# A two-layer decoder trunk on one core: the third down projection by halves, relu of one half on ScalarE, and steps moved between slots

## The chip, the core and the metric

The kernel runs on one core of one Trainium2 chip. The metric is the device time of one execution in microseconds (us). The kernel before took 1590.41 us as the median of three runs (1588.35 to 1590.41).

## What is computed

Two layers, each applied to a 512-token prompt and to 64 sampled tokens (8 sequences of 8), all in one pass over 576 columns. Everything is float32. Cut to what matters:

```
h = rms_norm(x, g_mix_pre)
proj = h @ w_in                      # 1024 -> 3584: queries, forget gates, values, gates of HGRN2; q, k, v of attention
rec, state = hgrn2(...)              # gated linear recurrence, 4 heads, chunks
att = dilated_attention(...)         # 8 heads, three (window, dilation) patterns, relative bias
x = x + rms_norm(concat(rec, att) @ w_out, g_mix_post)
h = rms_norm(x, g_mlp_pre)
u = square(relu(h @ w_up))           # 1024 -> 4096
x = x + rms_norm(u @ w_down, g_mlp_post)
```

Outputs: x of both groups after the last layer, the recurrent states, and the new rows of K and V.

## The kernel before, in words

Activations are transposed: features lie on the 128 partitions, tokens in the columns. The 576 tokens are cut in two halves of 320 and 256 columns, called half 0 and half 1 (`WIDE`). The weights come as blocks of 128x1024 float32 (512 KB). One block times one half gives one **output** of 128 features: 8 slices of 128 rows, each in three matmuls (high part of the weight, its rest, and the two parts of the activation), 24 matmuls in all, into one of two PSUM banks used in turn.

Each weight block passes a ring of four buffers (`RING`): SP loads it (`w_raw`), ScalarE copies it rounded (`high`, L770, tile `w_high`), VectorE subtracts (`rest`, L1400, tile `w_rest`); only the first blocks have their rest made elsewhere (GpSimd L694 for blocks 1 to 3). In steady state VectorE makes the rest of block v+4 right after the output that used block v, one output late.

The order of all work is written out by hand. `phases()` lists outputs in the order in which TensorE makes them; a layer is IA (input projection of half 0, 32 outputs), IB (half 1, 28 outputs, with OA, the output projection of half 0, in the middle), then the MLP. The MLP's 4096 hidden features are cut in four quarters: U0 to U3 are the up projections, D0 to D3 the down projections; A is half 0, B is half 1. The third down projection, D2, is done for both halves from one load of each block. The results of the D phases are summed in `acc[h]` (tile `reg`).

`steps_at()` hangs all other work on **slots**: slot (phase, i) is what every engine does after its part of output i. For each engine the program walks through the outputs and issues, per output, its eviction, the weight work and the slot's steps. So each engine's queue is in order, and a step that waits holds up what stands behind it. Steps that matter here:

- `norm_sum(k, h)`: sum over partitions on TensorE (L1109, ones), square root on ScalarE (L793), reciprocal on VectorE (L1424). k is 0 to 3: before the mixer, after it, before the MLP, after it.
- `post(k, h, p)`, p = 0 to 5: for two of eight slices, the projection's result times gain and norm (L1439), added to x (L1443); later p add up squares for the next norm (ScalarE L778, VectorE L1413).
- `pre(k, h, p)`: normalises x (L1455), rounds it (ScalarE L820 or L816, tile `h_high`), subtracts (L1467 or L1464, `h_rest`). For k = 2 the norm is left out here and multiplied in when the up projection is evicted.
- The eviction of an up output: VectorE, relu times the norm (L1497), then two squares on ScalarE (L872, L873) and a subtraction on VectorE (L1525). The norm factors of half 0 lie in `probs_s`, those of half 1 in `ks_tok` (`every_u`).
- `lev` and its helpers `q_odd`, `q_low`, `q_keep`, `q_rise`: levels of the recurrence (TensorE L1134, copies on ScalarE L890 and L897). `upd`: state update (VectorE L1664). `out`: the recurrence's output. `r_sum`, `r_spr`, `a_sum`, `a_spr`: norms per head (VectorE L1687, L1695). `sc`, `pt`, `pv`: attention (TensorE L1271, L1284, L1299).
- `x_sq`: squares of the input for the first norms. `f_scaled` (L1472): the first four outputs are made of x without its norm, and are multiplied by it afterwards.

## Time and profile before

| | |
|---|---|
| runs | 1588.35 to 1590.41 us, median 1590.41 |
| profiled execution, its own time | 1590.21 us |
| its span | 1588.4 us |
| what lies around the span | 1.8 us |
| TensorE matmul busy | 1535.0 us (97%) |
| VectorE busy | 1026.7 us (65%) |
| ScalarE busy | 806.6 us (51%) |
| DMA | 49% of 16 engines, 156 GB/s |

Times in the trace count from the start of the span. A busy TensorE is not TensorE at its peak; the start of each output against the next one tells whether it lost time.

### The profile page before, as it was taken

The page shows a single profiled execution, that of the slowest core. Times are in us where ns is not written, and L with a number is a line of the kernel's source. Part 1 is how long each engine was busy: PE and PEld are TensorE (multiplying, and loading weights), DVE is VectorE, ACT ScalarE, POOL GpSimd, SP SyncE. Part 2 cuts the span into 40 slices and gives each one's busy share as a digit, 9 for nine tenths or more (in the row PEclk, how much of TensorE's full clock was granted, in tenths as well). Part 3 has the DMA queues.
Part 4 walks back from the last instruction along what each step waited for, and adds up shares of the span by engine and source line. Part 5 has one row for each costly group of instructions (what it writes and reads, how often), then busy time and mean ns, then how long its engine had stood idle before and what let it go on. Part 6 is the DMA issues. An engine that isn't in the chain of part 4 may idle for free.

```text
span 1588.4 us, 29820 instructions
## 1 busy us (share of the span) xinstructions
PE 1535.0 (97%) x11984; PEld 1462.6 (92%) x11984; DVE 1026.7 (65%) x1784; ACT 806.6 (51%) x1424; POOL 124.6 (8%) x164
## 2 busy tenths in 40 slices
PE   6899999999999999999899999999999999999996
PEld 5898779998999999999899987899889999999996
DVE  6783777765558655445987656877555675653576
ACT  6545655476454644234664565546654454441442
POOL 3120123000000000000002100330000000000000
PEclk9999999999999999999999999999999999999998
DMA  5544664353454556334543467345434546652443
GB/s 202 187 152 164 216 224 130 123 179 107 133 170 147 172 181 183 119 107 146 160 146 120 139 214 260 127 145 159 153 93 147 160 153 182 184 172 80 138 154 113
DMA packets 83236, 247.88 MB, mean 156 GB/s; under 512 B 8691, under 2 KB 26483, under 8 KB 82972
## 3 DMA queue, kind: packets, MB, share of 16 engines
q1 hardware_dynamic: 83100, 245.98, 49.0%
q8 instruction: 96, 1.57, 0.4%
q14 instruction: 40, 0.33, 0.1%
HBM read 234.13 MB, written 14.44 MB: 156 GB/s over the span
## 4 chain that ended last, share of the span: by engine, by line
PE 81%; DVE 10%; ACT 3%; DMA 3%; issue 2%; SPq 1%; DVEq 0%; ACTq 0%
PE ps L1074 66%; PE ps L1071 6%; PE ps L1134 3%; DVE w_rest L1400 2%; DMA kc<-kcT 2%; PE ps L1284 1%; DVE reg L1439 1%; PE ps L1271 1%; PE ps L1299 1%; ACT w_high L770 1%; DVE x L1443 1%; DMA bias<-rel_scratch 1%; DVE square_sum L1413 1%; DVE norm_every L1424 1%; DVE s_in L1676 0%
## 5 line engine op out<-in xcount | busy, mean ns | idle before, releaser
L1074 PE MATMUL ps<-h_high,w_rest 128*128 128x320 f32 (+1 forms) x1888 | 569.4, 302 | 8.8 <-DVE w_rest L1400 4.7
L1074 PE MATMUL ps<-h_rest,w_high 128*128 128x320 f32 (+1 forms) x1888 | 559.8, 296 | 0.0
L1074 PE MATMUL ps<-h_high,w_high 128*128 128x320 f32 (+1 forms) x1888 | 559.7, 296 | 0.0
L770 ACT ACTIVATE w_high<-w_raw 128x1024 fp32r<-128x1024 f32 x384 | 402.1, 1051 | 224.1 <-PE ps L1074 223.2
L1400 DVE TENSOR_TENSOR w_rest<-w_raw,w_high 128x1024 fp32r<-128x1024 f32 x380 | 471.4, 1245 | 33.9 <-ACT w_high L770 33.8
L1074 PEld LDWEIGHTS ps<-h_high,w_rest 128*128 128x128 f32 x1888 | 359.6, 190 | 23.8 <-issue 14.1
L1074 PEld LDWEIGHTS ps<-h_rest,w_high 128*128 128x128 f32 x1888 | 359.8, 191 | 0.4
L1074 PEld LDWEIGHTS ps<-h_high,w_high 128*128 128x128 f32 x1888 | 359.5, 190 | 0.0
L1074 PE MATMUL ps<-u_high,w_rest 128*128 128x320 f32 (+1 forms) x1024 | 305.8, 299 | 3.8 <-DVE u_rest L1525 2.0
L1074 PE MATMUL ps<-u_high,w_high 128*128 128x320 f32 (+1 forms) x1024 | 303.4, 296 | 0.0
L1074 PE MATMUL ps<-u_rest,w_high 128*128 128x320 f32 (+1 forms) x1024 | 303.4, 296 | 0.0
L1074 PEld LDWEIGHTS ps<-u_high,w_rest 128*128 128x128 f32 x1024 | 194.8, 190 | 7.0 <-issue 4.2
L1074 PEld LDWEIGHTS ps<-u_rest,w_high 128*128 128x128 f32 x1024 | 194.8, 190 | 0.1
L1074 PEld LDWEIGHTS ps<-u_high,w_high 128*128 128x128 f32 x1024 | 194.7, 190 | 0.0
L872 ACT ACTIVATE tmp<-tmp 128x256 f32<-128x256 f32 (+1 forms) x128 | 57.0, 445 | 190.7 <-DVE tmp L1497 190.5
L1507 DVE TENSOR_TENSOR reg<-reg,ps 128x320 f32<-128x320 f32 (+1 forms) x96 | 43.5, 453 | 137.7 <-PE ps L1074 137.5
L1071 PE MATMUL ps<-w_rest,h_high 128*128 128x256 f32 (+1 forms) x320 | 93.9, 293 | 3.4 <-ACT key L857 2.7
L1497 DVE SCALAR_TENSOR_TENSOR tmp<-ps,probs_s 128x320 f32<-128x320 f32 x64 | 31.4, 490 | 94.3 <-PE ps L1074 94.3
L1071 PE MATMUL ps<-w_high,h_rest 128*128 128x256 f32 (+1 forms) x320 | 90.0, 281 | 0.0
L1071 PE MATMUL ps<-w_high,h_high 128*128 128x256 f32 (+1 forms) x320 | 90.0, 281 | 0.0
L1071 PEld LDWEIGHTS ps<-w_rest,h_high 128*128 128x128 f32 (+1 forms) x320 | 57.4, 179 | 7.7 <-issue 5.5
L1727 DVE CUSTOM_DVE_ANT_0 prob<-ps,bias 128x128 f32<-128x128 f32 (+3 forms) x64 | 28.7, 487 | 54.7 <-PE ps L1271 38.2
(203 smaller groups left out, 1673.8 us busy)
## 6 DMA issues: line engine op xcount, KB each, us to landing
w_raw<-w SPq DMA_DIRECT2D x384, 512.0 KB, 3.6
...
```

What stands on the lines that cost most here:

```text
L770: A.activation(whi[:, v % RING], raw[:, v % RING], ACT.Copy).then_inc(S["w_hi"], 1)
L872: A.activation(tmp[:, 2 + k % 2, 0:n], tmp[:, s, 0:n], ACT.Square)
L1071: last = pe.matmul(ps[0:rows, bank, 0:256].rearrange("p (s n) -> p s n", s=2), xt[:, c, t0:t0 + rows], wt[:, slot:slot + 2, c, :], **flags)
L1074: last = pe.matmul(ps[:, bank, 0:n], wt[:, slot, c, :], xt[:, c, :], **flags)
L1134: last = pe.matmul(ps[:, 3 + i, 256 * c:256 * c + 192].rearrange("p (z t) -> p z t", z=3), kb[h][:, 2 * g + i, pro(h, c)], qx[h][g][:, i, ...
L1271: last = pe.matmul(ps[:, 5 + s, b0 * P:(b0 + nb) * P], qa[h][r, j, pro(h, u % 2)], src[r, j, c0:c0 + nb * P], start=True, stop=True)
L1284: last = pe.transpose(dst, prob[h][:, s, j * P:j * P + P], ident)
L1299: last = pe.matmul(ps[DH * s:DH * s + DH, bank, c0:c0 + P], va[j // 2][:, j % 2, a * DH:a * DH + DH], pt[h][:, s, j * P:j * P + P], start= ...
L1400: V.tensor_tensor(wlo[:, v % RING], raw[:, v % RING], whi[:, v % RING].bitcast(F32), ALU.subtract).then_inc(S["w_lo_d"], 1)
L1497: V.scalar_tensor_tensor(tmp[:, gate_slot[o.n], 0:n], src, 0.0, every_u[o.h][:, 0:n], ALU.max, ALU.mult)\
L1507: V.tensor_tensor(dst, dst, src, ALU.add).then_inc(S["ev_d"], 1)
L1727: V.tensor_tensor_reduce(out=prob[h][:, s, 0:k], in0=ps[:, 5 + s, 0:k], in1=bias[h][j % 2][:, s, full - k:full], scale=1.0, scalar=-3.0e38 ...
```

## The change

1. **Phases.** U2B, D2, U3A, D3A, U3B, D3B become D2A, U3A, D3A, U2B, D2B, U3B, D3B. The eight blocks of D2 are loaded, rounded and subtracted twice per layer (400 blocks instead of 384). The last four phases belong to half 1 alone.
2. **The end of half 0's MLP.** `norm_sum(3,0)`, `post(3,0)`, `norm_sum(0,0)` and `pre(0,0)` are spread over these four phases, a step in every second slot, where they stood in every slot of U3B and D3B.
3. **Relu of half 1** goes to ScalarE (`ACT.Relu` from PSUM), without the norm; `pre(2,1)` normalises x on VectorE as for k = 0.
4. **Slots.** In IA, `norm_sum(0,1)` and `pre(0,1)` are issued behind the `q_` and `lev` steps of the same slot. In IB, `upd` of half 1 goes from slot 22 to 24 and `out` from 25 to 27. In D0A, `r_sum` and `r_spr` of half 1 start one slot later.
5. **The opening.** The square root's table is loaded ahead of the first squares by a dummy activation. Block 6 is rounded earlier (`N_SOON` 3). Outputs 2 and 3 are multiplied by the norm, and the rests of blocks 5 and 6 made, ahead of the forget gates' work. GpSimd makes no `h_rest` any more; VectorE does all. The squares of half 1's input move from slots 1 to 4 to slots 8 to 11.

```diff
-N_SOON = 2
+N_SOON = 3
...
-                                  ("U2B", "U", 2, (1,)), ("D2", "D", 2, (0, 1)), ("U3A", "U", 3, (0,)), ("D3A", "D", 3, (0,)),
-                                  ("U3B", "U", 3, (1,)), ("D3B", "D", 3, (1,))):
+                                  ("D2A", "D", 2, (0,)), ("U3A", "U", 3, (0,)), ("D3A", "D", 3, (0,)),
+                                  ("U2B", "U", 2, (1,)), ("D2B", "D", 2, (1,)), ("U3B", "U", 3, (1,)), ("D3B", "D", 3, (1,))):
...
-    put("IB", 22, "upd", 1)
+    put("IB", 24, "upd", 1)
-    put("IB", 25, "out", 1)
+    put("IB", 27, "out", 1)
...
-    put("D0A", 0, "r_sum", 1)
-    put("D0A", 1, "r_spr", 1, 0)
-    put("D0A", 2, "r_spr", 1, 1)
+    put("D0A", 1, "r_sum", 1)
+    put("D0A", 2, "r_spr", 1, 0)
+    put("D0A", 3, "r_spr", 1, 1)
...
-    put("U3B", 1, "norm_sum", 3, 0)
+    span = [(ph, i) for ph in ("U2B", "D2B", "U3B", "D3B") for i in range(KC)]
+    put(*span[1], "norm_sum", 3, 0)
     for p in range(6):
-        put("U3B", 2 + p, "post", 3, 0, p)
-    put("D3B", 1, "norm_sum", 0, 0)
+        put(*span[3 + 2 * p], "post", 3, 0, p)
+    put(*span[16], "norm_sum", 0, 0)
     for p in range(5):
-        put("D3B", 2 + p, "pre", 0, 0, p)
+        put(*span[18 + 2 * p], "pre", 0, 0, p)
...
+        if 8 <= o.i < 12:
+            here.append(("x_sq", 0, 1, o.i - 8))
...
-            for c in range(1, KC, 2):
-                pool.wait_ge(S["h_hi"], c + 1)
-                V.tensor_tensor(hl[0][:, c, :], first_x[:, c, :], hh[0][:, c, :].bitcast(F32), ALU.subtract).then_inc(S["h_odd"], 1)
...
+                elif o.kind == "U":
+                    s = (gates[0] + ups[0]) % 2
+                    if uses[s]:
+                        act.wait_ge(*uses[s])
+                    A.activation(tmp[:, s, 0:n], src, ACT.Relu).then_inc(S["ev_a"], 1)
...
             high(1)
+            A.activation(rn[:, 0:1], eps[:], ACT.Sqrt)
             for p in range(4):
                 x_sq(0, 0, p)
...
-                if p in (1, 4):
-                    rest(RING + p // 4)
+                if p == 1:
+                    rest(RING)
+            for o in outs[2:N_FIRST]:
+                f_scaled(o)
+            rest(RING + 1)
+            rest(RING + 2)
```

Three places show how queues change. In the names, `reg_55` is half 0's register tile and `reg_61` half 1's.

**VectorE, opening**, from the first reciprocal on. Before:

```order
L1424 RECIPROCAL norm_every<-norm_every 128x320
L1472 TENSOR_TENSOR tmp<-ps,norm_every 128x320 x2
L1455 SCALAR_TENSOR_TENSOR first_x<-x,prm,norm_every 128x320 x4
L1467 TENSOR_TENSOR h_rest_54<-first_x,h_high_53 128x320
L1400 TENSOR_TENSOR w_rest<-w_raw,w_high 128x1024
L1455 SCALAR_TENSOR_TENSOR first_x<-x,prm,norm_every 128x320 x2
L1467 TENSOR_TENSOR h_rest_54<-first_x,h_high_53 128x320
L1455 SCALAR_TENSOR_TENSOR first_x<-x,prm,norm_every 128x320 x2
L1467 TENSOR_TENSOR h_rest_54<-first_x,h_high_53 128x320 x2
L1400 TENSOR_TENSOR w_rest<-w_raw,w_high 128x1024
L1543 TENSOR_TENSOR lbc<-lb 128x4
```

Now:

```order
L1428 RECIPROCAL norm_every<-norm_every 128x320
L1474 TENSOR_TENSOR tmp<-ps,norm_every 128x320 x2
L1459 SCALAR_TENSOR_TENSOR first_x<-x,prm,norm_every 128x320 x4
L1469 TENSOR_TENSOR h_rest_54<-first_x,h_high_53 128x320 x2
L1404 TENSOR_TENSOR w_rest<-w_raw,w_high 128x1024
L1459 SCALAR_TENSOR_TENSOR first_x<-x,prm,norm_every 128x320 x2
L1469 TENSOR_TENSOR h_rest_54<-first_x,h_high_53 128x320 x2
L1459 SCALAR_TENSOR_TENSOR first_x<-x,prm,norm_every 128x320 x2
L1469 TENSOR_TENSOR h_rest_54<-first_x,h_high_53 128x320 x4
L1474 TENSOR_TENSOR tmp<-ps,norm_every 128x320 x2
L1404 TENSOR_TENSOR w_rest<-w_raw,w_high 128x1024 x2
```

The four subtractions of GpSimd have come in, and the last two rows hold the rests of blocks 5 and 6. Before, the rest of block 6 stood behind seven operations on `lbc` and `lb`, nine on three forget gates, three adds of squares, two copies and two `tmp` products.

**ScalarE, IA slots 13 to 15.** Before, then now:

```order
L820 ACTIVATE h_high_59<-reg_61 128x256 x2
L897 ACTIVATE q_mov_120<-reg_55 128x2x160
L890 ACTIVATE q_mov_119<-reg_55 128x2x128
L853 ACTIVATE reg_55<-ps 128x320
L770 ACTIVATE w_high<-w_raw 128x1024
```

```order
L893 ACTIVATE q_mov_119<-reg_55 128x2x128
L818 ACTIVATE h_high_59<-reg_61 128x256 x2
L856 ACTIVATE reg_55<-ps 128x320
L768 ACTIVATE w_high<-w_raw 128x1024
```

The copies into `q_mov`, for which `lev` waits, now stand ahead of the two roundings of `h_high`, which wait for VectorE's normalised x.

**VectorE, where half 0's `post(3,0)` begins.** Before (U3B), two slots:

```order
L1497 SCALAR_TENSOR_TENSOR tmp<-ps,ks_tok 128x256
L1400 TENSOR_TENSOR w_rest<-w_raw,w_high 128x1024
L1525 TENSOR_TENSOR u_rest_109<-tmp,u_high_107 128x256
L1439 SCALAR_TENSOR_TENSOR reg_55<-reg_55,prm,norm_every 128x320 x2
L1443 TENSOR_TENSOR x<-x,reg_55 128x320 x2
```

Now (U2B), two slots:

```order
L1404 TENSOR_TENSOR w_rest<-w_raw,w_high 128x1024
L1525 TENSOR_TENSOR u_rest_109<-tmp,u_high_107 128x256
L1443 SCALAR_TENSOR_TENSOR reg_55<-reg_55,prm,norm_every 128x320 x2
L1447 TENSOR_TENSOR x<-x,reg_55 128x320 x2
L1404 TENSOR_TENSOR w_rest<-w_raw,w_high 128x1024
L1525 TENSOR_TENSOR u_rest_109<-tmp,u_high_107 128x256
```

Before, every slot repeats all five rows; now the relu is gone from VectorE, and every second slot is without the `post`.

## Rows read from the trace of the kernel before

**Rows 1.** The page's first part: busy time, share of the span, instructions.
```profile
PE 1535.0 (97%) x11984; PEld 1462.6 (92%) x11984; DVE 1026.7 (65%) x1784; ACT 806.6 (51%) x1424; POOL 124.6 (8%) x164
```
**Rows 2.** TensorE's waits: line, whom it waited for, us in total, times, longest.
```profile
PE ps L1134 <- issue: 5.5, 8, 1.6
PE ps L1074 <- DVE w_rest L1400: 4.7, 1, 4.7
PE ps L1071 <- ACT key L857: 2.7, 2, 1.3
...
PE ps L1284 <- DVE reg L1695: 2.3, 2, 1.2
```
**Rows 3.** Stretches: length, busy PE, PEld, DVE, ACT, POOL, granted clock, DMA share, GB/s.
```profile
692.20:748.50 56.30, 56.30 (x386) 56.30 (x385) 30.00 (x44) 25.37 (x39) 0.00 (x0) 1.00 0.46 142
10.10:54.80 44.70, 36.73 (x199) 33.93 (x200) 36.35 (x69) 29.23 (x54) 14.15 (x9) 0.89 0.47 151
748.50:800.60 52.10, 48.11 (x390) 47.00 (x389) 48.09 (x85) 31.40 (x57) 0.00 (x0) 1.00 0.51 156
1526.00:1575.20 49.20, 47.59 (x388) 46.62 (x386) 36.47 (x62) 22.06 (x38) 0.00 (x0) 1.00 0.46 143
1303.30:1418.50 115.20, 115.20 (x962) 115.20 (x961) 70.46 (x104) 57.30 (x88) 0.00 (x0) 1.00 0.60 183
33.47:36.88 3.41, 3.27 (x12) 3.27 (x13) 3.13 (x9) 3.38 (x8) 0.95 (x1) 0.50 0.13 10
43.71:50.53 6.82, 5.22 (x19) 5.23 (x20) 6.42 (x14) 5.54 (x11) 0.00 (x0) 0.50 0.32 89
1166.70:1170.10 3.40, 3.40 (x15) 3.40 (x16) 0.48 (x1) 1.82 (x3) 1.28 (x1) 0.50 0.42 153
```
**Rows 4.** Timeline of the opening: start, us, engine, line, operation, tiles.
```profile
12.64 2.49 POOL L694 TENSOR_TENSOR w_rest<-w_raw,w_high 128x1024 fp32r<-128x1024 f32 x1 [10.39 <-ACT w_high L770]
...
13.25 2.24 DVE L1413 TENSOR_TENSOR square_sum<-squares 128x320 f32<-128x320 f32 x1 [0.38 <-ACT squares L778]
...
20.72 1.28 ACT L793 ACT_TABLE_LOAD   x1
...
22.58 2.15 DVE L1424 RECIPROCAL norm_every<-norm_every 128x320 f32<-128x320 f32 x1 [2.81 <-ACT norm_every L793]
...
25.57 1.93 DVE L1455 SCALAR_TENSOR_TENSOR first_x<-x,prm,norm_every 128x320 f32<-128x320 f32 x4
...
33.88 1.88 DVE L1400 TENSOR_TENSOR w_rest<-w_raw,w_high 128x1024 fp32r<-128x1024 f32 x1
...
44.04 1.22 DVE L1400 TENSOR_TENSOR w_rest<-w_raw,w_high 128x1024 fp32r<-128x1024 f32 x1
```
**Rows 5.** ScalarE's timeline in IA, first layer, slot 14.
```profile
89.79 0.81 ACT L820 ACTIVATE h_high<-reg 128x256 fp32r<-128x256 f32 x2 [2.44 <-DVE reg L1455]
```
**Rows 6.** Timeline in the second layer's IB, outputs 22 to 24.
```profile
1089.06 2.65 DVE L1664 SCALAR_TENSOR_TENSOR states<-states,f_tot,ps 128x128 f32<-128x128 f32 x8
...
1092.21 1.07 ACT L778 ACTIVATE squares<-x 128x320 f32<-128x320 f32 x2 [4.14 <-DVE square_sum L1413]
```
**Rows 7.** VectorE's timeline in U3B: the evictions of two neighbouring outputs.
```profile
762.66 0.42 DVE L1497 SCALAR_TENSOR_TENSOR tmp<-ps,ks_tok 128x256 f32<-128x256 f32 x1
...
766.19 0.42 DVE L1497 SCALAR_TENSOR_TENSOR tmp<-ps,ks_tok 128x256 f32<-128x256 f32 x1
```
**Rows 8.** Groups by line and form: busy us, mean ns | idle before.
```profile
L1109 PE MATMUL ps<-square_sum,ones 128*128 128x320 f32 x16 | 5.7, 437 | 0.7 <-DVE square_sum L1413 0.7
...
L857 ACT ACTIVATE key<-ps 128x256 f32<-128x256 f32 x8 | 3.0, 370 | 0.0
```
**Rows 9.** The page's costliest groups: weight rounding, weight rest, squares of up outputs.
```profile
L770 ACT ACTIVATE w_high<-w_raw 128x1024 fp32r<-128x1024 f32 x384 | 402.1, 1051 | 224.1 <-PE ps L1074 223.2
L1400 DVE TENSOR_TENSOR w_rest<-w_raw,w_high 128x1024 fp32r<-128x1024 f32 x380 | 471.4, 1245 | 33.9 <-ACT w_high L770 33.8
...
L872 ACT ACTIVATE tmp<-tmp 128x256 f32<-128x256 f32 (+1 forms) x128 | 57.0, 445 | 190.7 <-DVE tmp L1497 190.5
```

More of the change, by code:

```diff
@@ L99, in schedule @@
                 for j, (kind, h, k, tile) in enumerate(made):
-                    ev = EVICT[kind]
+                    ev = "a" if kind == "U" and h else EVICT[kind]
                     count[ev] += 1
@@ L117, in steps_at @@
         put("IA", 1 + p, "post", 3, 1, p)
-    put("IA", 13, "norm_sum", 0, 1)
-    for p in range(5):
-        put("IA", 14 + 2 * p, "pre", 0, 1, p)
     for G in range(GROUPS):
@@ L130, in steps_at @@
             put("IA", 9 + 4 * G + 2 * g, "lev", 0, G, g)
+    put("IA", 13, "norm_sum", 0, 1)
+    for p in range(5):
+        put("IA", 14 + 2 * p, "pre", 0, 1, p)
     put("IA", 18, "bias_in", 0, 0)
@@ L243, in steps_of @@
             if l == 0:
-                if name == "post" and which[2] < 4:
-                    here.append(("x_sq", 0, 1, which[2]))
                 continue
@@ L281, in scaled_before @@
     l, r = divmod(max(0, m - 2), 8)
-    return 8 * (m - 2 * l - (r > 1) - (r > 3))
+    return 8 * (m - l - (r > 1))
 def bank_of(o):
@@ L410, in build @@
     own_token = cst[:, 362:394]
-    every_u = [ps_s, kts]
+    every_u = ps_s
     def part(h, first):
@@ L788, in norm_sum @@
                 act.wait_ge(S["n_ms"], m + 1)
-                if k == 2:
-                    act.wait_ge(S["sp_t" if h == 0 else "su_done"], 4 * l + 4)
+                if (k, h) == (2, 0):
+                    act.wait_ge(S["sp_t"], 4 * l + 4)
                 elif m:
                     act.wait_ge(S["nap"], scaled_before(m))
-                A.activation((every_u[h] if k == 2 else every)[:, 0:WIDE[h]], ps[:, 7, 0:WIDE[h]], ACT.Sqrt, bias=eps[:], scale=1.0 / D)\
+                A.activation((every_u if (k, h) == (2, 0) else every)[:, 0:WIDE[h]], ps[:, 7, 0:WIDE[h]], ACT.Sqrt, bias=eps[:], scale=1.0 / D)\
                     .then_inc(S["n_root"], 1)
@@ L810, in pre @@
                 gain = prm[:, l, KC * k:KC * k + KC]
-                if k == 2 and p == 0:
-                    act.wait_ge(S["blk"], by[l, "OB" if h else "OA", KC - 1].n + 1)
+                if (k, h) == (2, 0) and p == 0:
+                    act.wait_ge(S["blk"], by[l, "OA", KC - 1].n + 1)
                 for c in (2 * p, 2 * p + 1):
-                    if k == 2:
+                    if (k, h) == (2, 0):
                         act.wait_ge(S["x_odd" if c % 2 else "x_even"], 4 * (4 * l + h) + p + 1)
@@ L828, in evict @@
                 src = ps[:, bank_of(o), 0:n]
-                if o.kind == "U":
+                if o.kind == "U" and o.h == 0:
                     return
@@ L867, in after @@
                     ups[0] += 1
-                    uses[s] = None
-                    act.wait_ge(S["ev_d"], o.evn)
+                    uses[s] = (S["u_sq"], ups[0])
+                    act.wait_ge(S["ev_a" if o.h else "ev_d"], o.evn)
                     if k >= 2:
@@ L1102, in _ @@
                      ("U0B", 0): normed, ("D0A", 0): upped, ("D0B", 0): upped, ("D1A", 0): upped, ("D1B", 0): upped,
-                     ("IA", N_FIRST): first_normed, ("D2", 0): upped, ("D2", 1): upped, ("D3A", 0): upped, ("D3B", 0): upped}
+                     ("IA", N_FIRST): first_normed, ("D2A", 0): upped, ("D2B", 0): upped, ("D3A", 0): upped, ("D3B", 0): upped}
             def norm_sum(l, k, h):
@@ L1421, in norm_sum @@
                 m, n = norm_no(l, k, h), WIDE[h]
-                to = (every_u[h] if k == 2 else every)[:, 0:n]
+                to = (every_u if (k, h) == (2, 0) else every)[:, 0:n]
                 dve.wait_ge(S["n_root"], m + 1)
@@ L1450, in pre @@
                 to = acc[h] if m else first_x
-                if p == 0 and k == 0:
+                if p == 0 and (k, h) != (2, 0):
                     dve.wait_ge(S["n_inv"], m + 1)
-                if p < 4 and k == 0:
+                if p < 4 and (k, h) != (2, 0):
                     for c in (2 * p, 2 * p + 1):
@@ L1458, in pre @@
                     for c in (2 * p - 2, 2 * p - 1):
-                        if m == 0 and c % 2:
-                            continue
                         dve.wait_ge(S["h_hi"], 8 * (4 * l + k + h) + c + 1)
                         done = S["h_odd" if c % 2 else "h_even"]
-                        if k == 2:
+                        if (k, h) == (2, 0):
                             V.scalar_tensor_tensor(hl[h][:, c, :], x[:, c, cols], gain[:, c:c + 1], hh[h][:, c, :].bitcast(F32),
@@ L1487, in evict @@
                     V.tensor_tensor(dst, src, tmp[:, gate_slot[o.n], 0:n], ALU.mult).then_inc(S["ev_d"], 1)
-                elif o.n in (2, 3):
-                    f_scaled(o)
-                elif o.kind == "U":
+                elif o.kind == "U" and o.h == 0:
                     k = n_up[0]
@@ L1496, in evict @@
                     dve.wait_ge(S["blk"], o.n + 1)
-                    V.scalar_tensor_tensor(tmp[:, gate_slot[o.n], 0:n], src, 0.0, every_u[o.h][:, 0:n], ALU.max, ALU.mult)\
+                    V.scalar_tensor_tensor(tmp[:, gate_slot[o.n], 0:n], src, 0.0, every_u[:, 0:n], ALU.max, ALU.mult)\
                         .then_inc(S["ev_d"], 1)
```

2 lines of the change are left out of this document (1 added, 1 removed).

## The prediction, made before the changed kernel had run

> **What bounds the kernel now.** The page's first part [rows 1] shows TensorE busy for 1535.0 us of 1588.4, VectorE 65%, ScalarE 51%. So a change counts only where TensorE now waits, or where it makes it wait. The next view is that of stretches [rows 3]. From 692.2 to 748.5, 16 outputs of half 0 take 56.3 us, 3.52 us each; from 1303.3 to 1418.5, 40 outputs of half 1 take 115.2 us, 2.88 us each, at full clock and 183 GB/s of loads. These two figures are the floor of an output: TensorE waits for nothing there. I hold every other stretch against them.
>
> Four kinds of places are above the floor. **The opening**: the first eight outputs take 44.7 us where the floor is 28.2, with one wait of 4.7 us for the rest of a weight block [rows 2, 3]. **Two places per layer in the mixer**: 1.6 us ahead of a `lev` (put down to issue; 5.5 us in 8 waits), and 1.3 us behind ScalarE's copy of a key (2.7 in 2) [rows 2]. **D0A**: 1.2 us behind `r_spr` on VectorE (2.3 in 2) [rows 2]. **U3B and D3B**: 52.1 us in the first layer and 49.2 in the second, where 16 outputs need 46.1 [rows 3]. There VectorE is busy 48.1 of 52.1 us. The clock is granted at 0.50, the lower level of 1.2 GHz, in three stretches of 3.4, 6.8 and 3.4 us [rows 3], each around a moment in which TensorE had been waiting (two in the opening, one in the second layer's D0A). At half clock half the time is lost: 5.1 us and 1.7 us.
>
> **The change part by part.**
>
> *The last four phases, 7.0 us.* In U3B a slot takes VectorE 3.53 us from one eviction to the next [rows 7] while TensorE needs 2.88: VectorE falls behind by 0.65 us in a slot, by 1 to 1.6 us where squares are added too, until the rests come late. Now the eviction (0.33 of it, by its record of 0.42 less the overlap with its neighbour) is ScalarE's, and the `post` stands in every second slot. The slot with it takes 3.2 us, the one without it 1.25 for the rest [rows 9] plus about 0.4 for the other subtraction, 1.65: 4.85 for two, 5.8 with two adds of squares of 0.48, where TensorE gives 5.76. VectorE just holds, with three outputs of reserve in the ring. So both stretches fall to the floor plus norm sums of 0.7 us each (5.7 us for 8 [rows 8]): 52.1 - 46.1 - 1.4 = 4.6 and 49.2 - 46.1 - 0.7 = 2.4. What is late next is nothing there; the tail after the last output keeps its chain.
>
> *Sixteen more block loads, nothing.* Each costs ScalarE 1.05 us and VectorE 1.25 us [rows 9]. They fall in D2A and D2B, where D2's outputs had a block for 6.4 us of TensorE. D2B then is like any B phase, whose 2.88 us per 512 KB block the stretch at 183 GB/s holds without a wait [rows 3]. Their cover is TensorE's own work; without it each would cost 1.25 us, 20 in all.
>
> *Relu on ScalarE, nothing.* It should last as long as the copy of a PSUM tile of the same form, 0.37 us [rows 8], against 0.42 on VectorE [rows 7]. ScalarE's turn in a half-1 up slot is then 1.05 + 0.37 + 2 x 0.45 = 2.3 us of 2.88 [rows 9], and 3.3 in every second slot of U2B with two squares more, 5.6 for two of 5.76. The step queued behind relu is the next block's rounding, needed three outputs later. The Trainium skill, "ScalarE: Activation LUTs", Rules for kernel authors, says to use VectorE for relu, per element up to about three times as fast in bf16; the float32 rows above show the two engines level, so here I leave it at nothing and keep the rule as a rival.
>
> *`pre(2,1)` normalised, nothing.* Eight products of about 0.48 us per layer on VectorE in U2A, four slots with 1.0 us more each. VectorE in comparable phases is busy 30.0 of 56.3 us [rows 3]. Bounds: 0 and 1 us per layer, if the last `h_rest` is late for U0B; the ring's reserve argues for 0.
>
> *`lev` ahead of `pre` in IA, 3.2 us.* ScalarE's roundings of `h_high` waited 2.44 us for VectorE and had the `q_mov` copies behind them [rows 5]; TensorE's wait of 1.6 us ended right after. With the copies first, they wait for nothing that is late. 2 x 1.6.
>
> *`upd` and `out` later in IB, 2.7 us.* The 2.65 us of state updates stood in front of the adds of squares, ScalarE's squares waited 4.14 us for these, and the key copy that frees TensorE's bank stood behind the squares [rows 6]. `upd` now comes behind the last of them. Gain between 0 (another wait in its place) and 2.7; I take 2.7, since slots 24 to 27 have less on VectorE.
>
> *`r_sum` and `r_spr` later in D0A, 4.0 us.* The last transposes (L1284) no longer stand behind the products that free their bank: 2.3 us [rows 2], and with the wait goes what I take to be the cause of the low clock from 1166.7 to 1170.1, worth 1.7 [rows 3].
>
> *The opening, 7.0 us.* The 1.28 us table load ahead of the square root at 20.72 goes [rows 4], so the reciprocal begins at 21.3 instead of 22.58. Where is the load now? Ahead of the first squares, which thereby come 1.3 us late. But the first add of squares, begun at 13.25, took 2.24 us and ended at 15.49, just after GpSimd's `w_rest` (12.64 to 15.13) [rows 4]: it did not get going earlier, and a start at 14.6 ends the same. The Trainium skill, "SBUF — State Buffer", section SBUF: two separate sides, calls this an exclusive lock on a port pair that VectorE and GpSimd share, held for a whole instruction; the trace agrees (2.24 us). Without such a lock the load would be paid and the opening gain 1.3 us less.
>
> From 21.3 on, VectorE's queue by the rows [rows 4]: reciprocal 2.15; two `tmp` and six more pieces of `first_x`, `h_rest` and `tmp` (8 `first_x`, 8 `h_rest`, 4 `tmp`, twenty operations, each taken at 1.93 / 4 = 0.48) 9.65; three block rests 3.75. The rest of block 5 is done at 35.6, of block 6 at 36.9. (Before: 35.8, and 45.3 for block 6, which is the wait of 4.7.) Four subtractions that were GpSimd's are in it. Output 5 runs from 35.6 at latest. If nothing else is late, outputs 5, 6 and 7 end at 35.6 + 3 x 3.52 = 46.1, where they ended at 54.8: 8.7 us. If the rest of block 7, behind 22 small operations, needs as long as the rest of block 6 did behind 23 (35.8 to 44.0, 8.3 us with its waits, and 1.25), it is there at 46.4, and the eighth output ends at 49.9: 4.9 us. I take 7.0. The low clocks are inside these times, except that TensorE again waits twice for over 1 us: one new stretch of 3.4 us at half clock would cost 1.7, and widens the low side. The squares moved to slots 8 to 11 lie under outputs with `lev` work between them; 0 to 1 us.
>
> **Sum**: 7.0 + 3.2 + 2.7 + 4.0 + 7.0 = 23.9 us. The profiled execution took 1590.2 us (span 1588.4 and 1.8 around it), 0.2 under the median of the runs, so the forecast is 1590.2 - 23.9, rounded to **1566 us**.
>
> **The rivals.**
>
> *The opening gives little* (20%). Its waits move to block 7 and the clock falls again. For: two waits of over 1 us remain by my own chain. Against: 4.9 us came out even with the long reading. With 1.5 instead of 7.0: 1571.5.
>
> *The mixer's waits come back behind the moved steps* (12%). `out` now stands right ahead of U0A, `r_spr` next to `a_sq`. Nothing is gained in IB and D0A, 6.7 us: 1573.
>
> *More than counted* (12%). VectorE is freer everywhere, and the records of neighbours overlap, so that my chains are long: 8.7 in the opening and some smaller waits: 1561.
>
> *Relu is slow on ScalarE* (3%). At three times VectorE's 0.42, 1.26 us, ScalarE's turn is 1.05 + 1.26 + 0.9 = 3.2 us, 0.33 over 2.88; 64 half-1 up outputs lose 21 us: 1587. The skill's rule, taken to the letter, is this case.
>
> *Slower* (4%). One mechanism: in the half-1 up phases ScalarE waits for VectorE's x and squares with the next output's relu queued behind, so that TensorE waits for its bank. It decides once ScalarE's turn, waits included, passes 2.88 us. At 3.35 us, 0.47 for 64 outputs, it costs 30 us, more than the 23.9: 1596. Against it: 0.6 us of room in the plain slots, and a reserve of one bank.
>
> *No change* (3%): the gains exist, but as waits that reappear before the MLP, whose floor they cannot lower: about 1590.
>
> *The forecast* has the remaining 46%. The range 1558 to 1577 takes in the first three rivals and the bounds above. A measurement of this kernel can tell 0.2%, 3 us, from no change. Faster by more than that: 0.93; within: 0.03; slower: 0.04.
>
> **What would show it.** The last four phases at 2.88 us per output and VectorE below 85% there, where it was 92%; no wait of 4.7 us on `w_rest`, and output 8 begun at 46 to 50 us instead of 54.8; no 1.6 us ahead of `lev`; no wait on `key` and `reg` L1695; granted clock 1.00 in D0A of the second layer. Wrong would be: waits on L1074 with ScalarE or VectorE named inside U0B to D1B, which have none now; or a low clock in a new place.

## The result

| | before | changed |
|---|---|---|
| runs | 1588.35 to 1590.41 us | 1569.68 to 1575.23 us |
| median of four runs each, same chip | 1589.87 us | 1570.07 us |
| profiled execution | 1590.21 us, span 1588.4 | 1569.68 us, span 1567.9 |

The ratio is 0.9887, with a 95% interval of 0.9867 to 0.9906. The span is 20.5 us shorter; the sum said 23.9. One execution of an experiment below took 2471.07 us, at a mean granted clock of 0.556; it is left out of every comparison.

The page's first part of the changed kernel answers to [rows 1]. ScalarE has 36.5 us more, TensorE 7.3 less.

```profile
PE 1527.7 (97%) x11984; PEld 1456.7 (93%) x11984; DVE 1031.7 (66%) x1756; ACT 843.1 (54%) x1501; POOL 120.7 (8%) x160
```

TensorE's waits after the change (line, whom it waited for, us in total, times, longest), against [rows 2]. The one of 4.7 us is gone, and so is that on `reg` L1695. New at the top stand two of 2.1 us on `w_rest` in L1075, a line that named ScalarE's `key` before; longer is only the wait of 10.3 us before the first output, which was 10.1 before.

```profile
PE ps L1075 <- DVE w_rest L1404: 4.3, 2, 2.1
PE ps L1138 <- issue: 3.1, 7, 0.9
PE ps L1078 <- DVE w_rest L1404: 2.4, 2, 1.3
...
PE ps L1318 <- DMA kc<-kcT: 1.6, 2, 1.2
...
PE ps L1366 <- ACT att_sq L993: 1.0, 2, 0.5
```

Stretches after the change (columns as in [rows 3]): the first eight outputs; the last four phases of layer 0; 16 outputs of U3B and D3B in layer 1; U0B to D1B in layer 1; D0A in layer 1; D2A in layer 1, where blocks are loaded that were shared before.

```profile
10.30:47.20 36.90, 32.93 (x199) 30.23 (x200) 31.09 (x66) 26.94 (x47) 8.43 (x5) 1.00 0.52 169
693.30:786.50 93.20, 93.20 (x775) 92.88 (x774) 73.28 (x112) 59.80 (x106) 0.00 (x0) 1.00 0.58 180
1508.60:1554.70 46.10, 46.10 (x385) 45.99 (x384) 24.98 (x35) 24.35 (x44) 0.00 (x0) 1.00 0.46 154
1285.30:1377.50 92.20, 92.20 (x771) 92.20 (x770) 51.71 (x65) 50.62 (x82) 0.00 (x0) 1.00 0.59 182
1136.90:1176.80 39.90, 39.41 (x308) 34.62 (x306) 21.99 (x37) 19.00 (x29) 3.87 (x3) 1.00 0.35 106
1377.50:1405.60 28.10, 28.10 (x194) 28.10 (x193) 12.93 (x16) 8.48 (x8) 0.00 (x0) 1.00 0.49 152
```

The last four phases take 2.91 us an output with VectorE at 79% (73.28 of 93.2), where U3B and D3B before had 3.26 and 92% [rows 3]. The granted clock is 1.00 in this execution until 1559.6 us; from there to the end it is 0.50, but TensorE has no work left (the kernel before has the same piece from 1579.7 us on).

Where the 20.5 us come from, by stretches between the starts of outputs in the two traces:

| stretch | before | changed | gain | forecast |
|---|---|---|---|---|
| IA, layer 0 | 149.6 | 140.8 | 8.8 | 7.0 + 1.6 |
| IA, layer 1 | 134.2 | 132.3 | 1.9 | 1.6 |
| IB slots 0 to 17, both layers | 199.5 | 198.7 | 0.8 | 0 |
| IB slots 18 to 27, both layers | 74.9 | 75.1 | -0.3 | 2.7 |
| U0A, both layers | 93.1 | 93.2 | -0.2 | 0 |
| D0A, layers 0 and 1 | 40.2 + 41.8 | 39.9 + 39.9 | 2.1 | 4.0 |
| U2B or D2A to D3B, layer 0 | 182.7 | 177.7 | 5.0 | 4.6 |
| the same, layer 1, with the tail | 192.9 | 190.4 | 2.5 | 2.4 |

All other phases agree within 0.1 us; the first output starts 0.1 us later. (Gains are taken before rounding.)

### The profile page after: what moved, and what is told of

It reads as the page before. It is cut to its first block, busy times and chain, and to the rows that moved or that the text cites. A ratio compares the mean times of both kernels' runs of the same rounds, so it can differ in the third digit from the quotient of the medians.

```text
span 1567.9 us, 29899 instructions
## 1 busy us (share of the span) xinstructions
PE 1527.7 (97%) x11984; PEld 1456.7 (93%) x11984; DVE 1031.7 (66%) x1756; ACT 843.1 (54%) x1501; POOL 120.7 (8%) x160
## 4 chain that ended last, share of the span: by engine, by line
PE 86%; DVE 8%; ACT 2%; DMA 2%; issue 1%; SPq 1%; DVEq 0%; ACTq 0%
PE ps L1078 68%; PE ps L1075 7%; PE ps L1138 3%; DVE w_rest L1404 2%; PE ps L1288 1%; PE ps L1303 1%; PE ps L1275 1%; DMA kc<-kcT 1%; DVE reg L1443 1%; ACT w_high L768 1%; DVE norm_every L1428 1%; DVE x L1447 1%; DVE s_in L1676 1%; DMA w_raw<-w 1%; PE ps L1193 0%
## 5 line engine op out<-in xcount | busy, mean ns | idle before, releaser
L768 ACT ACTIVATE w_high<-w_raw 128x1024 fp32r<-128x1024 f32 x400 | 419.0, 1052 | 208.9 <-PE ps L1078 206.5
L1404 DVE TENSOR_TENSOR w_rest<-w_raw,w_high 128x1024 fp32r<-128x1024 f32 x396 | 490.5, 1244 | 55.2 <-ACT w_high L768 55.1
L1078 PE MATMUL ps<-u_high,w_rest 128*128 128x256 f32 (+1 forms) x1024 | 304.9, 298 | 0.0
L1078 PE MATMUL ps<-u_high,w_high 128*128 128x256 f32 (+1 forms) x1024 | 303.1, 296 | 0.0
L1078 PE MATMUL ps<-u_rest,w_high 128*128 128x256 f32 (+1 forms) x1024 | 303.1, 296 | 0.0
L1075 PE MATMUL ps<-w_rest,h_high 128*128 128x256 f32 (+1 forms) x320 | 93.7, 293 | 4.3 <-DVE w_rest L1404 4.3
L1075 PE MATMUL ps<-w_high,h_rest 128*128 128x256 f32 (+1 forms) x320 | 90.0, 281 | 0.0
L1075 PE MATMUL ps<-w_high,h_high 128*128 128x256 f32 (+1 forms) x320 | 90.0, 281 | 0.0
L1525 DVE TENSOR_TENSOR u_rest<-tmp,u_high 128x256 fp32r<-128x256 f32 (+1 forms) x128 | 58.2, 455 | 38.3 <-ACT u_high L876 38.3
```

The source lines that it names most:

```text
L768: A.activation(whi[:, v % RING], raw[:, v % RING], ACT.Copy).then_inc(S["w_hi"], 1)
L1075: last = pe.matmul(ps[0:rows, bank, 0:256].rearrange("p (s n) -> p s n", s=2), xt[:, c, t0:t0 + rows], wt[:, slot:slot + 2, c, :], **flags)
L1078: last = pe.matmul(ps[:, bank, 0:n], wt[:, slot, c, :], xt[:, c, :], **flags)
L1404: V.tensor_tensor(wlo[:, v % RING], raw[:, v % RING], whi[:, v % RING].bitcast(F32), ALU.subtract).then_inc(S["w_lo_d"], 1)
L1525: V.tensor_tensor(ul[o.h][:, o.k, :], tmp[:, 2 + k % 2, 0:n], uh[o.h][:, o.k, :].bitcast(F32), ALU.subtract).then_inc(S["u_set"], 1)
```

## The experiments

The kernel before was run beside each experiment, and a ratio is to it. No experiment's interval lies apart from the changed kernel's, so the totals alone settle nothing. While TensorE has work, a granted clock of 0.50 shows in these traces in pieces of 3.4 us (once 6.8), none to four in one execution. So stretches of the traces are compared, and what a piece costs is named. The stretches repeat well: where D0A is not edited it takes 39.9 us in every layer of every compared trace of the new kernels.

### Relu and the spread, one without the other

All else as changed. First: the old phases, `post(3,0)` and `pre(0,0)` in every slot, with relu on ScalarE.

```diff
-                                  ("D2A", "D", 2, (0,)), ("U3A", "U", 3, (0,)), ("D3A", "D", 3, (0,)),
-                                  ("U2B", "U", 2, (1,)), ("D2B", "D", 2, (1,)), ("U3B", "U", 3, (1,)), ("D3B", "D", 3, (1,))):
+                                  ("U2B", "U", 2, (1,)), ("D2", "D", 2, (0, 1)), ("U3A", "U", 3, (0,)), ("D3A", "D", 3, (0,)),
+                                  ("U3B", "U", 3, (1,)), ("D3B", "D", 3, (1,))):
...
-        put(*span[3 + 2 * p], "post", 3, 0, p)
+        put("U3B", 2 + p, "post", 3, 0, p)
...
-        put(*span[18 + 2 * p], "pre", 0, 0, p)
+        put("D3B", 2 + p, "pre", 0, 0, p)
```

> The changed kernel (1570.1 us, span 1567.9) with the old phases: D2 for both halves from one load, post and pre of half 0 in every slot of U3B and D3B; relu stays on ScalarE. Theory A, spreading is what filled the gap in the last phases: a slot with post is 3.2 us of VectorE and 3.6 to 4.2 with adds of squares, against 2.88, on top of the reciprocal, so waits of 1 to 3 us per layer are back: span 1570 to 1573. Theory B, taking relu off VectorE was enough, since the ring holds a reserve of three outputs: span 1567.9 within 0.5, and 16 fewer block loads.

Second: the new phases, with relu and norm of half 1 on VectorE in one product.

```diff
-    A.activation(tmp[:, s, 0:n], src, ACT.Relu).then_inc(S["ev_a"], 1)
...
+    V.scalar_tensor_tensor(tmp[:, gate_slot[o.n], 0:n], src, 0.0, every_u[o.h][:, 0:n], ALU.max, ALU.mult)
```

> The changed kernel with relu of half 1 back on VectorE (norm multiplied in at the eviction, pre(2,1) without it); split and spreading stay. Theory A, spreading did it: two slots are 5.8 + 0.66 = 6.5 us against 5.76, six or so slots long, 2 us behind, inside the reserve: span 1567.9 within 0.5. Theory B, both are needed: waits in U2B to D3B of over 1 us per layer, span 1570 or more. If relu on ScalarE costs something where I counted nothing, the span is below 1567.5.

Measured: 1576.90 us, ratio 0.9913 (0.9893 to 0.9934), and 1574.19 us, 0.9905 (0.9891 to 0.9920). The stretches from U2B or D2A to the end of the layer:

| | layer 0 | layer 1 |
|---|---|---|
| neither (before) | 182.7 | 192.9 |
| relu moved alone | 181.1 | 190.8 |
| spread alone | 178.1 | 190.4 |
| both | 177.7 | 190.4 |

The spread alone gives 7.1 us, relu alone 3.7, both 7.5. With relu alone VectorE is still behind at the end of U3B: in the first output of D3B, layer 0, TensorE waits 2.4 us for the last up output's rest, and VectorE is busy 45.63 of 50.60 us in U3B and D3B (waits; stretch):

```profile
PE ps L1077 <- DVE u_rest L1524: 2.4, 1, 2.4
```
```profile
742.50:793.10 50.60, 47.91 (x391) 47.00 (x389) 45.63 (x77) 34.27 (x65) 0.00 (x0) 1.00 0.53 162
```

So in the first experiment theory A holds in layer 0; layer 1 is only 0.4 us longer than with both. In the second, theory A holds: without relu's move 0.4 us is lost, in layer 0 alone. Both spans (1574.9 and 1572.2 us) lie above what was written, with two pieces of low clock each, all in IB, where neither edit works.

Relu's price on each engine: ScalarE's group in the changed kernel (mean 384 ns), VectorE's in the second experiment (mean 420):

```profile
L847 ACT ACTIVATE tmp<-ps 128x256 f32<-128x256 f32 x64 | 24.6, 384 | 52.6 <-PE ps L1078 52.5
```
```profile
L1492 DVE SCALAR_TENSOR_TENSOR tmp<-ps,ks_tok 128x256 f32<-128x256 f32 x64 | 26.9, 420 | 46.9 <-PE ps L1073 46.9
```

They are close to level for float32 out of PSUM, 128x256, though VectorE's also multiplies by the norm. The Trainium skill, "ScalarE: Activation LUTs", Rules for kernel authors, prefers VectorE for relu, with a factor of up to about three per element that it gives for bf16. These float32 rows show no such lead: 384 ns on ScalarE against 420 on VectorE.

### IB: where `upd` and `out` stand

`upd` back in slot 22 and `out` in 25; then `upd` in slot 18, `out` left in 27.

```diff
+    put("IB", 22, "upd", 1)
...
-    put("IB", 24, "upd", 1)
-    put("IB", 27, "out", 1)
+    put("IB", 25, "out", 1)
```

> The changed kernel with upd and out of half 1 back in IB slots 22 and 25. Theory A, VectorE has more work than TensorE between IB 18 and 27, so that the wait has only changed its place: the waits of before (0.4 on w_rest and 1.35 on the key copy, per layer) replace the one of 2.1, span 1567.3 to 1568.2. Theory B, the step was worth moving and another cause made the new wait: it is slower by 2.7, span 1570.6.

> The changed kernel with upd of half 1 in IB slot 18, ahead of norm_sum(1,0), where VectorE stood idle for 2.6 us waiting for the root. Theory A (sum of VectorE's work): the 2.65 us fall in large part into that idle time, the reciprocal comes 1 to 1.6 us later, and the wait of 2.1 us per layer shrinks to about 1: span 1565.5 to 1567. Theory B (a delay of the reciprocal delays everything behind it in full, or TensorE waits for the token transposes): span 1568 or more.

The first: 1568.92 us (1568.34 to 1569.64), ratio 0.9872 (0.9857 to 0.9887). Slots 18 to 27 take 37.4 us, as before the change; the two short waits per layer are back (0.35 us on `w_rest`, 1.35 on `key`), the one of 2.13 is gone:

```profile
PE ps L1075 <- ACT key L860: 2.7, 2, 1.4
...
PE ps L1075 <- DVE w_rest L1404: 0.7, 2, 0.4
```

The move changed a wait for another, as theory A has it. Its span was written as 1567.3 to 1568.2 us and came out at 1566.5; 0.5 of that is the opening, which is late in the changed kernel's own trace (see there).

The second has no stretches to compare: its trace is of the execution left out above. The others took 1568.33, 1572.50 and 1575.07 us, which decides nothing between its theories.

VectorE's timeline of the changed kernel in layer 0, slots 22 to 24 (against [rows 6]):

```profile
299.09 1.22 DVE L1404 TENSOR_TENSOR w_rest<-w_raw,w_high 128x1024 fp32r<-128x1024 f32 x1
300.22 1.08 DVE L1417 TENSOR_TENSOR square_sum<-square_sum,squares 128x320 f32<-128x320 f32 x2
301.22 1.01 DVE L1443 SCALAR_TENSOR_TENSOR reg<-reg,prm,norm_every 128x320 f32<-128x320 f32 x2
302.15 0.89 DVE L1447 TENSOR_TENSOR x<-x,reg 128x320 f32<-128x320 f32 x2
302.95 1.22 DVE L1404 TENSOR_TENSOR w_rest<-w_raw,w_high 128x1024 fp32r<-128x1024 f32 x1
...
308.35 2.65 DVE L1664 SCALAR_TENSOR_TENSOR states<-states,f_tot,ps 128x128 f32<-128x128 f32 x8
```

TensorE waits until 304.27 for the rest begun at 302.95, and the state updates come only at 308.35: the wait ends ahead of them. VectorE has had no idle moment since its reciprocal at 289.03. From one rest to the next it needs 3.9 us (299.09 to 302.95) where TensorE gives 2.88. Two more edits asked what takes the wait away. First `upd` earlier and in two pieces:

```diff
+    put("IB", 18, "upd", 1)
+    put("IB", 19, "upd_b", 1)
...
-    put("IB", 24, "upd", 1)
...
-                for a in range(HR):
+                for a in (heads or (range(2) if h else range(HR))):
```

> upd of half 1 issued in slot 18 of IB, ahead of the posts with squares, and VectorE's eight state updates (2.65 us) cut in two: four in slot 18, four in slot 19; out stays in slot 27; all else as changed. In the changed kernel the eight stand together in slot 24 and slots 18 to 27 take 37.6 us with one wait of 2.13 us on w_rest per layer. Theory A (2.65 us of VectorE in one piece are what makes the weight rest late, and slots 18 and 19, whose posts have no squares, have 1.3 us of room each): the wait is gone, nothing over 0.6 us in its place, slots 18 to 27 at 35.5 to 36.3, no fall of the clock there, in all -2.6 to -4.2 us against a changed kernel without low clocks (1568), so about 1565. Theory B (VectorE's sum over slots 18 to 27 is the bound, so the wait only changes its place again): 37.2 to 37.8 and no gain. The two waits are in separate layers and should come out alike.

1574.47 us, ratio 0.9916 (0.9899 to 0.9933). Slots 18 to 27: 38.2 us, and 39.6 with a piece of low clock in it. The waits:

```profile
PE ps L1076 <- DVE w_rest L1405: 4.8, 2, 2.4
```

Theory A falls: with nothing of `upd` near slot 24 the wait there is longer, 2.4. Theory B fits, though 38.2 is 0.4 above its upper end: slot 18 grew by 1.8 us, since TensorE's part of `upd` now stands there. Last, the steps behind it moved back by a slot, with the transfer of the next section late as well:

```diff
-        put("IB", 18 + p, "post", 1, 0, p)
+        put("IB", 18 + p + p // 4, "post", 1, 0, p)
...
-        put("IB", 24 + (p + 1) // 2, "pre", 2, 0, p)
-    put("IB", 26, "norm_sum", 2, 0)
+        put("IB", 25 + (p + 1) // 2, "pre", 2, 0, p)
+    put("IB", 27, "norm_sum", 2, 0)
```

> The changed kernel with upd in slot 24 and out in slot 27, in which post 4 and 5 of half 0 stand one slot later in IB (23 and 24 instead of 22 and 23), the pre steps and the norm sum behind them one slot later too, and the transfer into rel_scratch in slot 9 as in the version just measured. In the changed kernel VectorE is busy without a gap from 289.0 to 311.9 and idle for 2.9 us from 311.9 on; TensorE waits 2.13 us on w_rest at 304.3. Theory A (VectorE's sum over slots 18 to 23 is too large by about 2 us, while slots 25 to 27 have room): the wait shrinks to under 1.0 us, slots 18 to 27 take 35.7 to 36.6 us instead of 37.6 in both layers, the first output of U0A does not wait, in all -2 to -4 us from here and -0.6 from slot 11 against the changed kernel's 1567.9 span: about 1564. Theory B (the sum over slots 18 to 27 is the bound, with the first output of U0A as its deadline): the wait shrinks but comes back in slot 27 or at the start of U0A, and the sum of both stretches stays within 0.5 us of 84.2 (37.6 and 46.6). Theory C (the pre steps pushed back cost more than the wait): U0A begins later by 1 us or more in all.

1571.60 us, ratio 0.9887 (0.9871 to 0.9904). Slots 18 to 27: 37.4 and 38.9 us (the latter with low clock), U0A 0.3 us longer in each layer. The waits:

```profile
PE ps L1075 <- DVE w_rest L1404: 4.3, 2, 2.1
```

None of the three theories was right: the wait is the same to 0.01 us. I had missed that `post` 4 and 5 hold only adds of squares, which stand behind the rest that TensorE waits for. The load is `post` 0 to 3 and the reciprocal, in slots 18 to 21, and they stayed. That moving those would help is argued, not shown.

What the first edit does show: with `upd` in slot 22, TensorE has 1.7 us of work of its own there (the slot takes 4.59 us instead of 2.88), and VectorE's rest is late by 0.35 instead of 2.13. `upd` brought its own cover, and the change moved the cover away together with the load.

### IA: `lev` behind `pre` again

```diff
+    put("IA", 13, "norm_sum", 0, 1)
+    for p in range(5):
+        put("IA", 14 + 2 * p, "pre", 0, 1, p)
...
-    put("IA", 13, "norm_sum", 0, 1)
-    for p in range(5):
-        put("IA", 14 + 2 * p, "pre", 0, 1, p)
```

> In IA the norm sum and the pre steps of half 1 issued ahead of the q and lev steps of the same slot again, as before the change; all else as changed. Theory A (the order of the copies on ScalarE against the roundings of h_high cost 1.6 us per layer): slot 15 goes from 5.39 back to about 7.0 in both layers, +1.6 to +1.8 us each, +3.2 to +3.6 in all, 1573 us. Theory B (slot 15 is short because the opening runs otherwise, or the later slots give it back): under +1 us in all. The second layer, where the opening has no part, tells them apart: +1.6 against 0.

1575.55 us, ratio 0.9916 (0.9900 to 0.9932). Slot 15 takes 7.03 and 7.24 us, where the changed kernel has 5.39 in both layers: 3.5 in all, and 3.7 with slots 13 and 14. TensorE's wait ahead of `lev` is back:

```profile
PE ps L1138 <- issue: 5.8, 9, 1.6
```

Theory A holds. ScalarE's timeline with the old order, then as changed: the roundings wait for VectorE either way, but the second `q_mov` begins at 83.53 in the one and at 81.09 in the other, with both kernels' output 15 begun within 0.7 us.

```profile
82.45 0.81 ACT L818 ACTIVATE h_high<-reg 128x256 fp32r<-128x256 f32 x2 [2.23 <-DVE reg L1459]
...
83.53 0.40 ACT L893 ACTIVATE q_mov<-reg 128x256 f32<-128x256 f32 x1
```
```profile
81.09 0.41 ACT L893 ACTIVATE q_mov<-reg 128x256 f32<-128x256 f32 x1
83.15 0.81 ACT L818 ACTIVATE h_high<-reg 128x256 fp32r<-128x256 f32 x2 [1.65 <-DVE reg L1459]
```

### D0A: `r_sum` and `r_spr` a slot earlier again

```diff
-    put("D0A", 1, "r_sum", 1)
-    put("D0A", 2, "r_spr", 1, 0)
-    put("D0A", 3, "r_spr", 1, 1)
+    put("D0A", 0, "r_sum", 1)
+    put("D0A", 1, "r_spr", 1, 0)
+    put("D0A", 2, "r_spr", 1, 1)
```

> In D0A the r_sum and r_spr steps of half 1 one slot earlier again, as before the change; all else as changed (D0A takes 39.9 us in both layers, clock 1.00; before the change 40.2 and 41.8, with the clock at 0.50 for 3.4 us in the second). Theory A (the wait of 1.2 us on r_spr is what lets the clock fall): D0A +0.3 us in the first layer and +0.3 to +1.9 in the second, with the low clock from the same place in some executions; in all +0.6 to +2.2. Theory B (the low clock came from waits earlier in that layer, in the state updates, which upd and out have moved away): the wait of 1.2 us is back, +0.6 in all, and the clock stays at 1.00 in D0A. If the wait on att_sq of 0.5 us goes at the same time, its 0.5 us are already inside these figures.

1574.46 us, ratio 0.9910 (0.9893 to 0.9927). The wait is back in both layers, and the clock falls right behind it in layer 0 (waits; stretches around it):

```profile
PE ps L1288 <- DVE reg L1695: 2.3, 2, 1.2
```
```profile
380.80:382.48 1.68, 0.53 (x8) 0.31 (x5) 1.65 (x4) 0.21 (x1) 0.00 (x0) 1.00 0.18 22
382.49:385.91 3.42, 3.42 (x17) 3.42 (x16) 0.32 (x1) 1.82 (x3) 1.28 (x1) 0.50 0.40 147
```

D0A takes 41.8 and 40.2 us against 39.9: 0.25 for the wait alone, 1.6 more with the clock. Theory A holds: in the kernel before it was layer 1 that lost the clock, here layer 0, each time behind this wait; in the 22 layers of the eleven compared traces without the wait it never fell in D0A. Of the 1.15 us of a wait 0.5 came back in the changed kernel as one on `att_sq`. The other 0.4 is no wait: without its waits D0A takes TensorE 39.0 us in this experiment (40.17 less 1.15) and 39.4 in the changed kernel (39.92 less 0.49). Why the same matmuls stand 0.4 us further apart stays open.

### The opening, one edit at a time

Three parts undone, each alone: the table load ahead of the squares, the squares of half 1's input out of the opening, the subtractions away from GpSimd.

```diff
-            A.activation(rn[:, 0:1], eps[:], ACT.Sqrt)
```

> The changed kernel without the dummy square root ahead of the first squares; all else as changed (1569.7 to 1575.2 us, profiled span 1567.9; output 8 begins at 47.15, the first layer's stretch of slots 0 to 31 of IA takes 140.8 us). Theory A (the load of 1.28 us lies on the chain first squares, square root, reciprocal): the reciprocal begins about 1.3 us later, output 8 at about 48.4, and the stretch takes 142.1: in all +1.3 us, 1571. Theory B (VectorE's queue or the weight loads set the opening, whatever the square root does): output 8 still at 47.2 and +0 to +0.3 us. Theory C (the dummy load itself delays the first squares on the chain of GpSimd and VectorE by as much as it saves): -1 to 0 us.

```diff
+                if name == "post" and which[2] < 4:
+                    here.append(("x_sq", 0, 1, which[2]))
...
-        if 8 <= o.i < 12:
-            here.append(("x_sq", 0, 1, o.i - 8))
```

> The squares of half 1's input back in the four slots of the opening (with post 0 to 3, outputs 1 to 4) instead of slots 8 to 11; all else as changed. In the changed kernel output 8 begins at 47.15 and slot 11 of IA took 6.51 us where it took 5.39 before. Theory A (the squares in slots 8 to 11 are what makes slot 11 longer): slot 11 back at 5.4, 1.1 us less there, while the three adds of squares, 0.5 us each, come back into VectorE's queue of the opening and make output 8 later by 1 to 1.5 us: in all -0.1 to +0.4. Theory B (the longer slot 11 comes from the weight load, which is late by 2.0 us there since the opening runs faster against the same DMA): slot 11 keeps 6.0 to 6.5, output 8 is later by 0.5 to 1.5 us and the whole is +0.5 to +1.5 us.

```diff
+            for c in range(1, KC, 2):
+                pool.wait_ge(S["h_hi"], c + 1)
+                V.tensor_tensor(hl[0][:, c, :], first_x[:, c, :], hh[0][:, c, :].bitcast(F32), ALU.subtract).then_inc(S["h_odd"], 1)
```

> The four subtractions h_rest of the odd slices of half 0 back on GpSimd in the opening; all else as changed (output 8 begins at 46.6 to 47.2 in the changed kernel and its sisters; in the kernel before at 54.8). Theory A (VectorE and GpSimd hinder each other, as with the first square_sum of 2.24 us, so that four subtractions given away gain nothing): VectorE's operations beside GpSimd's are longer by about what the four took, 1.9 us, output 8 at 46.5 to 48. Theory B (each engine for itself): VectorE has 1.9 us less to do ahead of the rests of blocks 5 and 6, the wait of 1.1 us on w_rest at output 5 and the one of 1.25 at output 7 shrink, output 8 at 45 to 46. Theory C (GpSimd is the slower and the products wait for it): output 8 at 49 or later, 2 us or more lost.

| undone | median, ratio (interval) | output 8 begins | slot 11 |
|---|---|---|---|
| nothing | 1570.07, 0.9887 (0.9867 to 0.9906) | 47.15 | 6.51 |
| table load ahead of the squares | 1575.30, 0.9915 (0.9898 to 0.9932) | 47.91 | 6.47 |
| squares moved to slots 8 to 11 | 1576.69, 0.9923 (0.9904 to 0.9943) | 50.18 | 6.18 |
| all subtractions on VectorE | 1572.55, 0.9898 (0.9883 to 0.9912) | 47.04 | 6.16 |

Eight other traces of versions with the same opening begin output 8 at 46.5 to 46.7. The changed kernel's own is 0.5 late: its second weight block landed at 12.0 us, in the version with the old order in IA at 10.2. Against 46.7, the table load is worth 1.2 us (theory A) and the squares 3.5. With the squares back, the last wait of the opening is 3.2 us instead of 1.3, and the clock falls at 45.5, worth 1.6 of the 3.5. Slot 11 stays long: theory B, though the price is over twice the 1.5 us that I wrote as its upper end. I had counted three adds of squares; seven come back, five of them (2.4 us) ahead of the rest that TensorE waits for. The waits on `w_rest` with the squares back:

```profile
PE ps L1078 <- DVE w_rest L1404: 4.3, 2, 3.2
```

GpSimd's four subtractions save VectorE nothing: from the reciprocal to the rests of blocks 5 and 6 it needs 12.4 us with four operations fewer, against 12.1 (21.20 to 33.59, 21.66 to 33.72), and output 8 is 0.4 late. With GpSimd at work (first fence, GpSimd then VectorE) two products take 1.63 us; in the changed kernel (second fence) the same two take 1.00.

```profile
27.67 1.63 POOL L760 TENSOR_TENSOR h_rest<-first_x,h_high 128x320 fp32r<-128x320 f32 x1 [0.59 <-ACT h_high L821]
...
28.49 1.63 DVE L1462 SCALAR_TENSOR_TENSOR first_x<-x,prm,norm_every 128x320 f32<-128x320 f32 x2
```
```profile
28.66 1.00 DVE L1459 SCALAR_TENSOR_TENSOR first_x<-x,prm,norm_every 128x320 f32<-128x320 f32 x2
```

Theory A holds. The Trainium skill, "SBUF — State Buffer", section SBUF: two separate sides, describes an exclusive lock on a port pair that the two engines share, held for the whole of an instruction. The rows agree with it (1.63 us against 1.00), but they show the slowing and not the lock itself.

### Slot 11: the transfer into `rel_scratch` later

On the version with `upd` in slot 22.

```diff
-        if o.i == 5:
+        if o.i == 9:
             here.append(("rel_all", 0))
-        if 9 <= o.i < 25:
-            here.append(("rel_tab", 0, o.i - 9))
+        if 13 <= o.i < 29:
+            here.append(("rel_tab", 0, o.i - 13))
```

> The version with upd back in slot 22 and out in slot 25 (1568.92 us, span 1566.5), and in it the transfer of 2560 KB into rel_scratch issued in slot 9 of IA instead of slot 5, its readers in slots 13 to 28 instead of 9 to 24. In that version slot 11 of IA took 6.02 us (6.2 to 6.5 in its sisters) with a wait ahead of lev, where 5.39 is enough. Theory A (the transfer shares the DMA engines with the weight loads just when the opening's outputs of 3.5 us ask for a block each, and makes the block of slot 11 late): slot 11 at 5.4, 0.6 to 1.1 us less, and in slots 13 to 17, which are longer, the transfer hides. Theory B (the delay comes from the ring of four buffers, which the faster opening empties before the loads catch up): slot 11 unchanged, 0. Theory C (the transfer only moves the wait): slot 11 at 5.4 and one of slots 13 to 17 longer by as much.

1568.72 us (1567.92 to 1569.93), ratio 0.9875 (0.9861 to 0.9890). Slot 11 takes 5.39 us and slots 13 to 17 are as they were: theory A. In the ten compared traces of the new kernels that have the transfer in slot 5 it takes 5.6 to 6.5 us; in this one, and in the one with the later `post` above, which has it in slot 9 too, 5.39. The block load issued right behind the transfer, at 49.5 us, lands after 12.8 us in the changed kernel; the same block's, at 49.0, after 3.9 with the later transfer. ScalarE's rounding of the block, in the changed kernel and with the later transfer:

```profile
62.32 1.06 ACT L768 ACTIVATE w_high<-w_raw 128x1024 fp32r<-128x1024 f32 x1 [2.00 <-DMA w_raw<-w]
```
```profile
59.75 1.05 ACT L768 ACTIVATE w_high<-w_raw 128x1024 fp32r<-128x1024 f32 x1
```

The median gained 0.2 us, less than its runs scatter; the profiled execution has a piece of low clock elsewhere (layer 1, at 978). This version and that with `upd` back are the fastest measured; neither is told apart from the changed kernel by its interval.

## Why the prediction was right, and where not

The forecast was 1566 us, the measurement 1570.07, inside the range and faster as said. By its steps:

- **The last four phases, 7.0: right, 7.5.** Both stretches fell to the floor plus the norm sums, which cost 0.5 us each instead of 0.7. The spread did most of it; relu's move adds 0.4 to the spread. VectorE "just holds" was too dark: 79%.
- **Sixteen more block loads, relu, `pre(2,1)`, nothing: right.** D2A runs without a wait (194 matmuls in 28.10 us), U2A is 28.6 in both, U0B to D1B keep their 92.2.
- **`lev` ahead of `pre`, 3.2: right,** 3.7 by undoing it.
- **The opening, 7.0: right in sum, in part by luck.** The first eight outputs gained 7.8 us (44.7 to 36.9) and slot 11 gave 1.1 back; 0.3 more came in the last slot of IA. By the rows of the two stretches, about 4.0 of the 7.8 is less idle time of TensorE and 3.8 less busy time, at a granted clock of 1.00 instead of 0.89. The prediction left the clock inside its times and priced a fall anew, with 1.7; none came. The squares, at 0 to 1 us of cost in my sum, were not the cause of the longer slot 11: the transfer into `rel_scratch` was, which I had not looked at. The table load paid 1.2 as reckoned: the reciprocal begins at 21.66 here and at 21.18 in the version with the old order in IA, against 21.3 reckoned.

VectorE's and ScalarE's timeline of the changed opening, against [rows 4]: the add of squares, 2.24 us before, now takes 0.62 and ends 0.5 later. That is the late second block; in the version with the old order in IA it ends at 15.52, within 0.1 of the 15.49 before, as the prediction said.

```profile
13.12 1.28 ACT L1020 ACT_TABLE_LOAD   x1
...
14.53 0.81 ACT L776 ACTIVATE squares<-x 128x320 f32<-128x320 f32 x2
15.38 0.62 DVE L1417 TENSOR_TENSOR square_sum<-squares 128x320 f32<-128x320 f32 x1 [2.38 <-ACT squares L776]
...
21.66 2.15 DVE L1428 RECIPROCAL norm_every<-norm_every 128x320 f32<-128x320 f32 x1 [1.38 <-ACT norm_every L791]
```

- **`upd` and `out` later, 2.7: wrong, 0.4 lost.** The step that failed: "I take 2.7, since slots 24 to 27 have less on VectorE". I read [rows 6] as a matter of order. But VectorE is behind before slot 24, and `upd` had given it time, since TensorE has 1.7 us of work on it too. Slots 18 to 27 lost 0.3 us and U0A 0.2, before rounding 0.4 together. It is my second rival in one of its two places: nothing gained, a wait in another's place.
- **`r_sum` and `r_spr` later, 4.0: half right, 2.1.** The clock part came (1.6 of 1.7). The wait part, 2.3, was mis-sized: 0.5, for the whole wait was counted and the next one, on `att_sq` (0.5 us), was not looked for.
- **Not forecast**: 0.8 us in IB slots 0 to 17, where waits for transfers of `kc` differ from execution to execution (2.5 us in all before, 1.6 here, 3.6 in another version).

Together: 7.0 + 3.7 + 7.5 + 2.1 - 0.4 + 0.8 = 20.7, against 20.5 by the spans; the first output starts 0.1 later. The sum forecast 23.9: two terms were 5.0 us too high (`upd`, `r_sum`), and 1.8 came back from terms that were too low or not there.
